# A two-layer hybrid decoder trunk in float32: when the first layer's S5 b matrices are fetched and spread, and where one step of the stick-breaking attention stands

## What is computed

```python
for l in range(DEPTH):
    h = rms_norm(x, norm_mix[l])
    u_ssm, q_nsa, kv_nsa, g_nsa, qkv_sb, g_merge = split_columns(h @ w_in[l])
    o_ssm = s5_mixer(u_ssm, ...)        # complex state space, 32 groups of 64 states
    o_nsa = nsa_mixer(rope(q), rope(k), v, gates, ...)
    o_sb = stick_breaking_attention(q, k, v)
    x = x + (sum(sigmoid(g_merge) * (branches @ w_branch)) @ w_out[l])
    x = x + conv_ffn(rms_norm(x, norm_ffn[l]), ...)
```

```python
bb_re = f_re * b_re - f_im * b_im
bb_im = f_re * b_im + f_im * b_re
```

## Time and profile before

| | us |
|---|---|
| runs shown | 946.54, 946.89, 948.06 |
| median | 946.89 |
| profiled execution | 950.34 |
| its span | 948.6 |
| TensorE busy | 925.0 |
| VectorE busy | 708.3 |
| ScalarE busy | 592.2 |
| GpSimd busy | 289.2 |

### The profile page before, as it was taken

One profiled execution on the slowest core, in us unless ns is written; L12 is line 12 of the kernel. 1 busy time (PEld: TensorE's weight loads), 2 busy tenths in 40 slices (PEclk: granted clock), 3 DMA queues, 4 the chain that ended last, 5 costly groups with the idle time before them and its releaser, 6 DMA issues.

```text
span 948.6 us, 16008 instructions
## 1 busy us (share of the span) xinstructions
PE 925.0 (98%) x5839; PEld 776.7 (82%) x5839; DVE 708.3 (75%) x1131; ACT 592.2 (62%) x956; POOL 289.2 (30%) x226
## 2 busy tenths in 40 slices
PE   8899999999999999999999999999999999999997
PEld 6889777777778888888879987777787788888886
DVE  6799967665667887898864977766657687777777
ACT  7445776768455765666665467677664566566655
POOL 0433324351420568467101413443316001010010
PEclk9999999999999999999999999999999999999999
DMA  9993433453554755556449844433645456556551
GB/s 221 247 269 98 147 123 132 132 150 129 167 176 138 219 192 193 177 185 213 139 123 264 233 154 134 133 117 106 180 131 178 133 178 207 193 177 205 191 179 45
DMA packets 139559, 159.09 MB, mean 168 GB/s; under 512 B 17153, under 2 KB 106089, under 8 KB 139498
## 3 DMA queue, kind: packets, MB, share of 16 engines
q1 hardware_dynamic: 137960, 156.44, 53.6%
q10 hardware_dynamic: 1538, 1.84, 0.7%
HBM read 154.33 MB, written 1.05 MB: 164 GB/s over the span
## 4 chain that ended last, share of the span: by engine, by line
PE 78%; DVE 9%; ACT 4%; SPq 3%; DMA 2%; issue 2%; ACTq 1%; POOL 0%; DVEq 0%; PEldq 0%; POOLq 0%
PE pj L801 57%; PE bX L801 7%; PE bA L801 6%; PE bB L801 4%; DVE wl L1733 3%; DMA ring<-in_w_in 2%; PE pj L1069 1%; ACT wh L1390 1%; SPq L618 1%; PE pj L1165 1%; SPq L671 1%; DVE gate L1758 1%; DVE s5a L1960 1%; DVE h L1765 1%; SPq L615 1%
## 5 line engine op out<-in xcount | busy, mean ns | idle before, releaser
L1733 DVE TENSOR_TENSOR wl<-ring,wh 128x1024 fp32r<-128x1024 f32 (+1 forms) x276 | 361.4, 1311 | 96.0 <-ACT wh L1390 94.8
L1390 ACT ACTIVATE wh<-ring 128x1024 fp32r<-128x1024 f32 (+1 forms) x276 | 288.2, 1045 | 154.4 <-PE pj L801 112.0
L801 PE MATMUL pj<-h,wh 128*128 128x256 f32 (+1 forms) x1376 | 296.6, 339 | 6.0 <-DVE wl L1733 5.0
L801 PE MATMUL pj<-wh,h 128*128 128x512 f32 (+1 forms) x832 | 259.6, 394 | 2.4 <-DVE h L1765 0.8
L801 PEld LDWEIGHTS pj<-h,wh 128*128 128x128 f32 x1376 | 230.6, 191 | 32.8 <-issue 7.0
L801 PE MATMUL pj<-h,wl 128*128 128x256 f32 x1024 | 189.0, 283 | 0.0
L801 PEld LDWEIGHTS pj<-wh,h 128*128 128x128 f32 x832 | 148.4, 188 | 41.5 <-issue 7.3
L801 PEld LDWEIGHTS pj<-h,wl 128*128 128x128 f32 x1024 | 157.6, 191 | 6.5
L801 PE MATMUL pj<-wl,h 128*128 128x512 f32 (+1 forms) x416 | 159.7, 384 | 0.0
L2422 POOL TENSOR_TENSOR work<-work 128x512 f32<-128x512 f32 x20 | 41.1, 2056 | 260.8 <-DVE work L2198 199.0
L801 PEld LDWEIGHTS pj<-wl,h 128*128 128x128 f32 x416 | 78.1, 188 | 16.3
(11 more groups left out here) (305 smaller groups left out, 1228.8 us busy)
## 6 DMA issues: line engine op xcount, KB each, us to landing
ring<-in_ffn_w_up SPq DMA_DIRECT2D x44, 1024.0 KB, 5.1
ring<-in_w_in SPq DMA_DIRECT2D x40, 1024.0 KB, 5.1
ring<-in_ffn_w_down SPq DMA_DIRECT2D x22, 1024.0 KB, 5.0
ring<-in_w_in SPq DMA_DIRECT2D x16, 512.0 KB, 5.5
ring<-in_w_branch SPq DMA_DIRECT2D x8, 1024.0 KB, 5.3
ring<-in_w_out SPq DMA_DIRECT2D x8, 1024.0 KB, 5.1
ring<-in_w_branch SPq DMA_DIRECT2D x8, 512.0 KB, 6.5
ring<-in_w_in SPq DMA_DIRECT2D x8, 256.0 KB, 3.4
```

The lines of the kernel that those rows point to most:

```text
L801: return nc.tensor.matmul(o, a, b, start=start, stop=stop, skip_group_check=True)
L1390: A(dst, src, ACT.Copy).then_inc(w_hi.sem, 1)
L1733: TT(dst, src, hi.bitcast(F32), ALU.subtract).then_inc(w_lo.sem, 1)
```

## The change

It has four edits.

1. The two b DMAs get a function of their own (`load_b`) and a semaphore of their own (`b_in`). In layer 0 they are issued behind chunk 8; for layer 1 they stay where they were. `mats_in` counts four DMAs instead of six.
2. `s5_b` on VectorE and its semaphore `b_made` are gone. In layer 0 GpSimd now runs `spread_b`, `products_ab`, `sums_ab` and `spread_ab` in one go behind its fourth rotary product. `spread_b` waits for `b_in`.
3. The sums of a stick-breaking pair become a function, `sb_softplus`. At the late gate the third pair's sums (k = 2) stand between the two gate copies; the other pairs' stay.
4. In layer 1's start VectorE's low part 1 stands behind the last `x_down` half and the second `turned_lo`.

```diff
+B_LATE = 8
@@ SyncE
             def load_mats(l):
-                for r, w in enumerate((ssm_b_re, ssm_b_im)):
-                    mat_in(bnat[:, r], row(w, l).rearrange("l (t w) p i -> (w p) (l t) i", w=2))
...
+                    if l == 0 and i == B_LATE:
+                        load_b(0)
...
                     load_rows(l + 1)
+                    load_b(l + 1)
                     load_mats(l + 1)
@@ VectorE
                     x_down(l - 1, 1, 0)
                     turned_lo(l, 1, 0, 0, 0)
-                    split_lo(l, 1)
                     x_down(l - 1, 1, 1)
                     turned_lo(l, 2, 0, 1, JC)
+                    split_lo(l, 1)
...
                 split_lo(l, 8)
-                if l == 0:
-                    s5_b()
                 split_lo(l, 9)
...
                                 .then_inc(unit_out[n % 2].sem, unit_out[n % 2].up())
+                            if t == 0:
+                                sb_softplus(SB_P[q + 1])
+                    if q in SB_P and q != GATE_LATE + 1:
+                        sb_softplus(SB_P[q])
@@ GpSimd
             def spread_b(l):
                 g.wait_ge(turns_ready.sem, 1)
+                g.wait_ge(b_in.sem, b_in.at(l, 16 * 2))
...
-                if l == 0:
-                    g.wait_ge(b_made.sem, 1)
-                    g.wait_ge(consts_in.sem, 16)
-                    spread(bb, l, 0).then_inc(bx_ready.sem, bx_ready.up())
-                    products_ab(l)
-                    sums_ab()
...
-                    if l == 0 and n == 1:
-                        spread_ab(l)
+
+                if l == 0:
+                    spread_b(l)
+                    products_ab(l)
+                    sums_ab()
+                    spread_ab(l)
```

More of the change, by code:

```diff
@@ L400, in build @@
         rows_in = sem("rows_in", 16 * 11)
-        mats_in = sem("mats_in", 16 * 6)
+        b_in = sem("b_in", 16 * 2)
+        mats_in = sem("mats_in", 16 * 4)
         params_free = sem("params_free", 1, 1)
@@ L431, in build @@
         bx_ready = sem("bx_ready", 2)
-        b_made = sem("b_made")
         cx_ready = sem("cx_ready", 2)
@@ L705, in load_rows, with load_b @@
                 par_in(stC[C_B:C_B + 2 * FT, :], row(ffn_conv_b, l).rearrange("l (k p) -> (l k) p", p=P))
+            def load_b(l):
+                for r, w in enumerate((ssm_b_re, ssm_b_im)):
+                    sp.dma_start(bnat[:, r], row(w, l).rearrange("l (t w) p i -> (w p) (l t) i", w=2))\
+                        .then_inc(b_in.sem, b_in.up(16))
             def load_mats(l):
-                for r, w in enumerate((ssm_b_re, ssm_b_im)):
-                    mat_in(bnat[:, r], row(w, l).rearrange("l (t w) p i -> (w p) (l t) i", w=2))
                 for r, w in enumerate((ssm_c_re, ssm_c_im)):
@@ L1393, in spread_c @@
             def spread_c():
-                a.wait_ge(mats_in.sem, mats_in.at(0, 16 * 6))
+                a.wait_ge(mats_in.sem, mats_in.at(0, 16 * 4))
                 a.wait_ge(consts_in.sem, 16)
@@ L1880, in table @@
                     stepped(TT(tn[:, :, n:2 * n], tn[:, :, n:2 * n], turned_both[:, 0], ALU.add))
[L1882 to L1889, removed]
             for l in range(DEPTH):
@@ L2084, in s5_scan, with sb_softplus @@
                     ins.then_inc(g5_ready.sem, g5_ready.up())
+                def sb_softplus(k):
+                    v.wait_ge(z_ln.sem, z_ln.at(l, k + 1))
+                    if k:
+                        v.wait_ge(r_done.sem, r_done.at(l, k))
+                    for e in range(2):
+                        ins = STT(sbp[:, e, 0:384], (bA, bB)[e][:, 0:384], 0.0, sbw[k % 2][:, e, 0:384], ALU.max, ALU.add)
+                    ins.then_inc(z_sp.sem, z_sp.up())
                 if l:
@@ L2270, in spread_c @@
             def spread_c(l):
-                g.wait_ge(mats_in.sem, mats_in.at(l, 16 * 6))
+                g.wait_ge(mats_in.sem, mats_in.at(l, 16 * 4))
                 for c, mask in enumerate((K_PAR, K_NPAR)):
```

## The result

The changed kernel took 950.53 us (median of 6 runs, 950.05 to 952.13), the kernel before 946.96 us beside it (6 runs, 946.54 to 949.3). The ratio is 1.0034, with a 95% interval of 1.0024 to 1.0044: 3.6 us slower. Both intervals lie above 1, so both say slower; the size lies between 1.5 and 3.6 us, and the two intervals overlap only from 1.0024 to 1.0028. The ratio beside it can say up to half a us more or less.)

What follows compares the result with a forecast made beforehand. The start was taken to be bound first by DMA, then by VectorE, with TensorE busy 98% of the span. Start +2.1, late gate -0.8, layer 1's start -0.4 gave +0.9 on 946.89: 947.8 us, range 943.3 to 952.6.

Steps and rivals of the forecast that it cites:

- piece 16 after 60: Sign of a wrong forecast: TensorE begins layer 0's half weight chunk 16 later than 60 us; 57 was expected.
- Part 1: Layer 0's start: b matrices asked for later, weight chunks arrive sooner, a head start of 5.6 us (bounds 2.4 and 6.8).
- Part 2: Layer 0's start: removing VectorE's four b steps gives 0, since VectorE still has time there.
- Part 3: Layer 0 behind the rotary: GpSimd's 18 moved instructions slow VectorE by 7.7 us (bounds 3.2 and 12.7).
- The start in sum: Layer 0's start up to half weight chunk 22: 7.7 us contention less 5.6 us head start, +2.1 us.
- 2 us or more at pieces 18, 19 and 22: Sign of a right forecast: TensorE waits this long for VectorE's low parts at these half weight chunks of layer 0.
- Part 4: Late gate, third stick-breaking pair: TensorE's 0.40 us wait for GpSimd's masking goes in each layer, -0.8 us.
- Part 5: Layer 1's start: last residual half done sooner, second row tile's norm transposes start earlier, -0.4 us.
- (a): Rival: VectorE and GpSimd hardly disturb each other, contention 3.2 us instead of 7.7, time 943.3 us; chance 0.22.
- (c): Rival: data still late, held up by bytes ahead in the queue; head start 2.4 us, time 951.0 us; chance 0.08.
- (b): Rival: VectorE stands for each of GpSimd's 18 instructions in full, 12.7 us, time 952.8 us; chance 0.16.
- (d): Rival: TensorE's clock falls at one of the new waits, up to 2 us more, 949.8 us; chance 0.08.

Runs made afterwards that it cites:

- the kernels without the reads: Changed kernel with GpSimd's 18 instructions on layer 0's b matrices replaced by one zero fill, 941.65 us, or by nine zero fills, 943.44 us.

## Why the prediction came out as it did

I forecast 947.8 us, +0.9 us, with "slower" at 0.40, "same" at 0.34; measured are +3.6 us and +1.5 us on two chips. Both lie within the range. The sign and the main mechanism were right (a head start from the late loads, more than eaten by the contention behind it); the size was a quarter of the first measurement and about half of the second. That it came this close is in part luck: the start was forecast 1.3 us too cheap and the two late parts 0.8 us too poor, and these errors offset each other. By my own list of signs not all went well either: "piece 16 after 60" was to mean that I was wrong, and piece 16 began at 61.56. Term by term:

- **Part 1, the head start: 5.6 us forecast, 4.96 us in the trace.** The step that was off is VectorE's pair of low parts 14 and 15. I let GpSimd rest beside them; it does its third rotary product there, and the pair took 3.45 us, as long as before. High part 12, too, still waits for its chunk. The price of 0.6 us is in the change's disfavour. And I put all of it down to the loads. By the traces they are worth 3.1 to 4.3 us, and 0.69 us is what the four spreads had cost VectorE's rotary steps in before, which my sum held without saying so ("2.3 us when GpSimd rests").
- **Part 2, no gain from VectorE's four steps.** It wasn't tried alone. The traces show no gain from these four; the second edit's gain ahead of low part 14 comes from GpSimd's spreads, not from them.
- **Part 3, the contention: 7.7 us forecast, 8.36 us in the trace** (8.25 us against the kernels without the reads). The sum of 0.36 us for a short instruction and 0.97 us for a wide one was 8% low: a spread costs 0.39 us by experiment. GpSimd began at 53.4, not 55.8, and was done by 69.8, not 78, so the wait for the matrices never came near. One reading behind the sum was wrong: the low part at 82.56 didn't lie beside one wide GpSimd instruction but beside two (82.19 to 83.67 and 83.64 to 85.91), so 0.97 us was the price of parts of both. That the two wide ones of the 18 cost about 1.0 us each all the same is an estimate from the kernel with the spreads on ScalarE.
- **The start in sum: +2.1 forecast, +3.36 at piece 22.** TensorE's waits are not where I put them. I let the price fall at pieces 18 to 22, but the first eight block copies and two rotary steps, which low part 16 stands behind, already lay beside GpSimd. So TensorE's own pace, "piece 16 at 57.0", never counted; with the work left out it does begin at 57.72. I expected 2 us or more at pieces 18, 19 and 22; it waits 5.35 us at piece 16, 0.68 us at piece 19, and 2.15 us + 0.61 us ahead of piece 22. Of that the 2.15 us is ScalarE's: its copies of the b operands stand in its order behind an exponential that needs VectorE's softmax.
- **Part 4, the late gate: -0.8 forecast, -1.34 in the trace, -1.4 measured alone.** The mechanism was right. The size was the profile's idle figure, 0.40 us a layer, and a bubble is worth more than that. In before the last matmul ahead of the wait starts at 222.06, with the next due 0.23 us behind it; the one that waits starts at 222.84, 0.55 us later than that, and is 0.10 us slower (1.14 against 1.04 us). The figure of 0.40 leaves out the 0.16 us that the pipelined matmul takes longer than its pace. So 0.65 us for each 0.40 shown.
- **Part 5, layer 1's start: -0.4 forecast, -0.65 in the trace.** Same mechanism: the earlier trace rows shows a wait of 0.56 us ahead of the transposes, and after none.
- **Rivals.** (a), cheap contention, and (c), data still late, fall by the traces. (b), full exclusion, was to cost 12.7 us, and to decide from 8.7 us on; the price is 8.3 us, under both, though closer to the line than the forecast was. (d), the clock, came true: 0.50 behind the wait at piece 16 and 0.57 behind the one at piece 22. As a cost it is 0.2 us in the traces of the changed kernel and 1.4 to 1.5 us in three other kernels whose clock fell there too, so (d) is part of the answer and not a rival to it. Two small slips: the upper end of the range, 952.6, leaves out (b)'s 952.8, and the 0.43 us for each short instruction at 8.7 us is 0.42.

What was right in the kernel is the part nobody would call the main one: the two late reorderings give all the gain, 1.9 us, and the start takes 3.2 us.

Open: why the whole change is +3.6 us on one chip and +1.5 us on another. The parts are consistent on the second and third; the first comparison has 6 runs of before, and no other kernel was run on that chip. The time that the low clock behind piece 22 takes differs by over 1 us between executions, which may be a part of it; that isn't shown.

## What to carry to other kernels

Before work is moved to an engine that "has time", ask where its new place lies against the engine it shares SBUF reads with: the 18 instructions cost 8.3 us where VectorE was the bound, while the 12 of them that GpSimd had done earlier, mostly where VectorE waited for data, show only 0.69 us on the way to low part 15. Masked or scaled copies can go to ScalarE where it waits: here four took 1.7 us, and moving eight gave 3.0 us back. And price a short wait of TensorE by the distance between the starts of its matmuls, since the idle figure of the profile gave 0.40 us for what was worth 0.65.

## What the runs showed of the hardware

- **Short two-input instructions of VectorE pass GpSimd's one for one.** Eight block copies of 0.24 us each took 4.58, 5.52, 6.18 and 7.17 us beside GpSimd's two-input instructions, while a low part of 1.22 us took 1.63 to 2.31 us. Taken one by one in after, the first eight copies lie beside seven GpSimd instructions: seven copies take 0.61 to 1.36 us, and one, which starts just ahead of a GpSimd instruction, 0.28 us. The second eight lie beside six, and two of them take 0.28 us. A copy and a short product together take 0.62 us (the products start at 53.42, 54.04, 54.66), less than the 0.24 + 0.60 us that they take apart; 0.62 - 0.24 = 0.38 us is the loss, as the 0.39 us by experiment.
- **A fill on GpSimd costs VectorE's two-input instructions nothing**: 14.90 us of fills, and the block copies stayed at 1.93 us. One instruction with a single input was held up, 1.27 us for 0.18 us.
- **A wait of TensorE can go on costing time behind it.** Behind the wait ahead of piece 22 the granted clock fell to 0.50, and the time lost by 130 us was 0.2 us in two traces and 1.4 to 1.5 us in three.
- **A small transfer can hold the issuing queue for long.** The b matrices are 0.13 MB each; the second held SyncE's queue 3.43 us early and 5.63 to 7.07 us behind chunk 8 (six kernels), where three chunks are issued right ahead of it. Behind chunk 7 it held it 7.58 us; behind chunk 6 5.36 us, and high part 14 waited 2.60 us for chunk 7. The two c matrices, of the same size, held it 0.51 to 2.83 us, so it is not the bytes alone; what else it is wasn't tested.
